# Four moved pieces in a two-block transformer kernel: order of turns in latent attention, low parts of the convolution branch on VectorE, a sum inside a tile, and the first weights between blocks of x

## The reference, cut to what matters

```python
def first_block(x, ...):
    h = rmsnorm(x, norm_in_g)                       # the prologue of the kernel
    proj = h @ w_in                                 # first weight tiles of the ring
    ... stick-breaking attention: y_sb ...
    q = (rmsnorm(c_q) @ w_q_up)                     # 8 heads, 64 + 32 columns each
    kv = (rmsnorm(c_kv) @ w_kv_up)                  # 8 heads, 64 for k and 64 for v
    z = q_full @ k_full.T * scale                   # per head, queries in blocks of 128
    p = softmax(where(allowed, z, -inf))            # key chunk <= query chunk
    o_mla = p @ v_mla
    x = x + (g0 * y_sb + g1 * ((o_mla * silu(gate_mla)) @ w_o_mla)) @ w_out
    return rmsnorm(x, norm_f_g)

def second_block(x, ...):
    ... differential attention a and a causal convolution c of 31 taps ...
    y_a = a @ w_proj_attn
    c = silu(layer_norm(c, conv_ln_w, conv_ln_b))
    y_b = c @ w_proj_conv
    x = x + (sigmoid(g_a) * y_a + sigmoid(g_b) * y_b) @ w_out
    ... feed-forward with silu gate ...
```

## Time and profile before

| | |
|---|---|
| median of three runs | 3171.05 us |
| the profiled execution's own time | 3167.18 us |
| span of its profile | 3165.4 us |
| mean granted TensorE clock | 0.967 of full |
| TensorE busy | 2899.7 us (92%) |
| VectorE busy | 1580.2 us (50%) |
| ScalarE busy | 1228.4 us (39%) |
| GpSimd busy | 750.1 us (24%) |

### The profile page before, as it was taken

The page is one execution under the profiler, slowest core; times in us unless marked ns, Lnnn a source line. Parts: engine busy times, 40 slices in busy tenths (PEclk is TensorE's granted clock), DMA queues, the critical chain, the costliest instruction groups (busy, mean ns, idle before and its releaser), DMA issues. The chain is left out here.

```text
span 3165.4 us, 34002 instructions
## 1 busy us (share of the span) xinstructions
PE 2899.7 (92%) x13392; PEld 2344.9 (74%) x13392; DVE 1580.2 (50%) x1934; ACT 1228.4 (39%) x2019; POOL 750.1 (24%) x330
## 2 busy tenths in 40 slices
PE   6999998977778888999999999978989999999999
PEld 4778887756666766777777777766777888888887
DVE  4566664145675343788888877745332221211121
ACT  4455543224453243565566555535124110111110
POOL 2111121110001231333333333216223222222221
PEclk8999999988999998999999999989999999999999
DMA  4112122113213421211221122244430111111112
GB/s 118 34 54 60 47 67 86 41 28 65 45 37 129 144 80 50 80 46 58 67 62 55 55 67 68 67 179 140 138 115 20 47 47 51 49 47 47 47 47 80
DMA packets 239286, 219.16 MB, mean 69 GB/s; under 512 B 29304, under 2 KB 200856, under 8 KB 239128
## 3 DMA queue, kind: packets, MB, share of 16 engines
q1 hardware_dynamic: 238096, 215.41, 22.1%
q10 hardware_dynamic: 1032, 1.57, 0.3%
HBM read 156.66 MB, written 41.42 MB: 63 GB/s over the span
## 5 line engine op out<-in xcount | busy, mean ns | idle before, releaser
L179 POOL TENSOR_TENSOR w_lo<-w_raw,w_hi 128x1024 fp32r<-128x1024 f32 (+3 forms) x220 | 515.9, 2347 | 1905.6 <-ACT w_hi L171 1905.6
L171 ACT ACTIVATE w_hi<-w_raw 128x1024 fp32r<-128x1024 f32 (+3 forms) x220 | 215.6, 983 | 610.1 <-PE f_banks L239 203.1
L2213 DVE SCALAR_TENSOR_TENSOR d_acc<-d_padded,vectors,d_acc 128x1024 f32<-128x1024 f32 x240 | 389.8, 1624 | 3.0
L209 PE MATMUL d_pp<-h_hi,w_hi 128*128 128x512 f32 x896 | 362.4, 404 | 11.1 <-PEq L67 4.5
L209 PE MATMUL d_pp<-h_hi,w_lo 128*128 128x512 f32 x896 | 362.2, 404 | 0.0
L209 PE MATMUL d_pp<-h_lo,w_hi 128*128 128x512 f32 x896 | 359.9, 402 | 0.0
L239 PE MATMUL f_banks<-h_hi,w_hi 128*128 128x512 f32 x704 | 222.2, 396 | 4.5 <-PEq L67 4.5
L239 PE MATMUL f_banks<-h_lo,w_hi 128*128 128x512 f32 x704 | 221.7, 395 | 0.0
L239 PE MATMUL f_banks<-h_hi,w_lo 128*128 128x512 f32 x704 | 221.6, 395 | 0.0
L209 PE MATMUL s_pp<-h_hi,w_hi 128*128 128x512 f32 x512 | 206.5, 403 | 12.7 <-PEq L67 12.7
L1992 POOL TENSOR_TENSOR d_probs<-d_probs 128x128 f32<-128x128 f32 (+3 forms) x64 | 133.6, 2088 | 338.0 <-ACT d_probs L2108 338.0
(11 more groups left out here) (338 smaller groups left out, 5861.8 us busy)
## 6 DMA issues: line engine op xcount, KB each, us to landing
w_raw<-in_w_in SPq DMA_DIRECT2D x97, 512.0 KB, 3.9
w_raw<-in_w_gate_up SPq DMA_DIRECT2D x44, 512.0 KB, 3.8
w_raw<-in_w_down SPq DMA_DIRECT2D x22, 512.0 KB, 3.6
gates<-s_gate SPq DMA_DIRECT2D x16, 512.0 KB, 5.1
f_gate<-gates SPq DMA_DIRECT2D x16, 512.0 KB, 4.8
w_raw<-in_w_out SPq DMA_DIRECT2D x16, 512.0 KB, 3.7
w_raw<-in_w_proj SPq DMA_DIRECT2D x16, 512.0 KB, 4.9
x_tok_in<-in_x SPq DMA_DIRECT2D x8, 512.0 KB, 7.8
```

The lines of the kernel that those rows point to most:

```text
L171: act.activation(self.hi[:, s, 0:chunks, :], self.raw[:, s, 0:chunks, :], ACT.Copy).then_inc(self.rounded[s], 1)
L179: pool.tensor_tensor(self.lo[:, s, 0:chunks, :], self.raw[:, s, 0:chunks, :], f32(self.hi[:, s, 0:chunks, :]), ALU.subtract).then_inc(self ...
L209: mm = pe.matmul(halves(ps)[h], w[:, k, :], x[:, k, h * HALF:(h + 1) * HALF], start=(k == 0 and r == 0), stop=(k == chunks - 1 and r == 2))
L2213: dve.scalar_tensor_tensor(out=acc[:, :], in0=x, scalar=wt, in1=acc[:, :], op0=ALU.mult, op1=ALU.add).then_inc(c["taps"], 1)
```

## The change

Prologue: SyncE issues the two first weight tiles behind block 3 of x in place of behind block 7, and ScalarE rounds them inside round 7 of its loop, ahead of the last two `h_hi`.

Latent attention: in each step but the second of a head (`at == 1`) the turns of unit s-2 come straight behind the scores, ahead of `fill` and `values`; in the second (`LATE`) they stay behind `values`. The turns of v come at the fifth step (`at == 4`) in place of the seventh, and last in it. ScalarE's roundings and VectorE's subtractions are put in the same order, and so is the numbering `order` of the two banks.

`merge_branches`: the low parts of the convolution's result go from GpSimd (between its tiles 6 and 7 and after 7) to VectorE (all eight in round 6); ScalarE rounds them four at a time one round later than before, apart from the sigmoids; the sum over rows of the squares stands inside tile 4, behind its second chunk, in place of behind tile 3; the reloads of the attention's result are issued one round later.

```diff
-        CONV_V = 6
+        CONV_V, LATE = 4, 1
...
@@ latent attention, ScalarE
+                turned_here = [(s - 2, x) for x in range(CHUNKS[(s - 2) % QB])] if 2 <= s < UNITS + 2 else []
+                if at != LATE:
+                    for u, x in turned_here:
+                        round_t(u, x)
                 if s < UNITS:
                     expose(s)
                 for t, h in halves_at(s):
                     take(t, h)
                 if s >= LAG and (s - LAG) % 2 == 1:
                     copy_low((s - LAG) // 2)
+                if at == LATE:
+                    for u, x in turned_here:
+                        round_t(u, x)
+                if at == CONV_V and head < HEADS_:
+                    for x in range(2):
+                        round_v(head, x)
...
@@ latent attention, TensorE
                 if s < UNITS:
                     score(s)
+                if at != LATE:
+                    for u, x in turned_here:
+                        turn_t(u, x)
                 for t, h in halves_at(s):
                     fill(t, h)
                 if s >= LAG and (s - LAG) % 2 == 1:
                     values(s - LAG)
+                if at == LATE:
+                    for u, x in turned_here:
+                        turn_t(u, x)
                 if at == CONV_V and head < HEADS_:
                     for x in range(2):
                         turn_v(head, x)
-                if 2 <= s < UNITS + 2:
-                    for x in range(CHUNKS[(s - 2) % QB]):
-                        turn_t(s - 2, x)
...
@@ prologue
-            ring.load_ahead(sp)
+                if b == 3:
+                    ring.load_ahead(sp)
...
-            ring.round_ahead(act)
+                if b == TB - 1:
+                    ring.round_ahead(act)
...
@@ merge_branches
-                if u in (5, 7):
+                if u in (6, 8):
...
-                if t in (6, 7):
-                    for k in range(4):
-                        low(k + (4 if t == 7 else 0))
...
+                if t in (5, 6):
+                    for k in range(4):
+                        round_c(k + (4 if t == 6 else 0))
...
+                if t == 6:
+                    for k in range(KC):
+                        low(k)
...
+                    if (t, k) == (4, 1):
+                        pe.wait_ge(c["square_sum"], KC - 1)
+                        add_over_rows(sum2, c["squares_summed"])
```

More of the change, by code:

```diff
@@ L951, in latent_attention @@
             head, at = s // QB + 1, s % QB
+            if 2 <= s < UNITS + 2:
+                order += [("t", s - 2, x) for x in range(CHUNKS[(s - 2) % QB])]
             if at == CONV_V and head < HEADS_:
                 order += [("v", head, 0), ("v", head, 1)]
-            if 2 <= s < UNITS + 2:
-                order += [("t", s - 2, x) for x in range(CHUNKS[(s - 2) % QB])]
         number = {what: i for i, what in enumerate(order)}
@@ L1205, in _ @@
                     norm(s - 1)
[L1206 to L1211, removed]
+                turned_here = [(s - 2, x) for x in range(CHUNKS[(s - 2) % QB])] if 2 <= s < UNITS + 2 else []
+                if at != LATE:
+                    for u, x in turned_here:
+                        low_t(u, x)
                 for t, h in halves_at(s):
@@ L1215, in _ @@
                     add_low((s - LAG) // 2)
+                if at == LATE:
+                    for u, x in turned_here:
+                        low_t(u, x)
+                if at == CONV_V and head < HEADS_:
+                    for x in range(2):
+                        low_v(head, x)
         @block.tensor
@@ L2607, in _ @@
                     invert()
+                if t in (5, 6):
+                    for k in range(4):
+                        round_c(k + (4 if t == 6 else 0))
                 if t in (4, 5):
-                    for k in range(4 * (t - 4), 4 * (t - 4) + 4):
-                        sigmoid_of(k)
-                        if k % 4:
-                            round_c(k - 1)
-                    round_c(4 * (t - 4) + 3)
+                    for k in range(4):
+                        sigmoid_of(k + (4 if t == 5 else 0))
             ring.round_ahead(act)
@@ L2647, in product, with low @@
                                          op0=ALU.add, op1=ALU.mult).then_inc(c["product"], 1)
+            def low(k):
+                dve.wait_ge(c["rounded"], k + 1)
+                dve.tensor_tensor(c_lo[:, k, :], x[:, k, :], f32(c_hi[:, k, :]), ALU.subtract).then_inc(c["low"], 1)
             for k in range(KC):
```

15 lines of the change are left out of this document (1 added, 14 removed).

## The result

The changed kernel takes 3142.18 us (median of four runs, 3140.68 to 3143.81), the kernel before 3169.71 us beside it. The ratio on record is 0.9902, 95% interval [0.9889, 0.9915]: faster by about 1%, where -15 us was forecast. The two medians are 27.5 us apart, which is 0.9913 and inside that interval; 0.9902 itself would be 31 us, and the record does not say where these 3.6 us come from. The profiled execution took 3140.68 us with a span of 3138.9, 26.5 less than before.

What follows compares the result with a forecast made beforehand. TensorE was taken as the bound, busy 2899.7 of 3165.4 us. Prologue +21.5, `merge_branches` -16.5 and latent attention -20 sum to -15.0 us, so 3156 us from a median of 3171.05; range 3132 to 3172.

Steps and rivals of the forecast that it cites:

- Rival (1): Prologue: it doesn't lengthen, since block 4 of x lands early; -38.5 us in all, 3132.5 us; chance 0.12.
- The 1.1 us taken off: `merge_branches`: deducted from its 17.6 us gain because GpSimd's remaining w_lo can stretch VectorE's low parts; left -16.5.
- The "third": `merge_branches`: GpSimd's w_lo can stretch VectorE's low parts by a third, as 2.34 became 3.33 us in the prologue.
- The 5 us taken off: Latent attention: deducted because a waiting turn holds up the half tile, the values and their takers; left -20 us.
- Heads 2 to 5: Latent attention: the longer of two engines' sums per step plus 2.5 us slack per head, a gain of 21 us.
- Heads 1 and 6: Latent attention: a gain of 4 us for both together.
- Heads 7 and 8: Latent attention: nothing changes, as their step is VectorE's.
- The upper end, -34: Latent attention: if heads with half tiles ran like head 7, 28 us less in heads 2 to 5, some 5 elsewhere.
- (2): Latent attention gives only -8 us, as its waits become waits of the turns; total -3, 3168 us; chance 0.17.
- (3): Latent attention: early turns couple the engines, 0.5 us in each of 64 steps; total +12, 3183 us; chance 0.11.
- the likeliest case: Whole kernel: the forecast itself, 3156 us, with its own range of 3143 to 3166; chance 0.60.
- the two signs set for a wrong forecast: Block 4 taken up before 30 us, or the turns' waits in latent attention 20 us more than before.

Runs made afterwards that it cites:

- pro_alone: The kernel before with the prologue's edit alone; 3193.68 us, 1.0071 of the kernel before.
- bias_later: The changed kernel with ScalarE issuing the bias rows in round 4 of the prologue, not before its loop; 3122.73 us, 0.9842 of the kernel before.
- mer_sum3: `no_pro` with the sum over rows of the squares back behind tile 3 in `merge_branches`; 3122.91 us in one run.
- pe_half_last: `no_pro` with TensorE alone turning behind half tile and values in steps with a half tile; 3134.58 us, 0.9875 of the kernel before.
- turns_only: The kernel before with TensorE alone turning right behind the scores in every step, v still at the seventh; 3152.62 us, 0.9931 of the kernel before.
- pe_half_early: `no_pro` with TensorE alone turning behind the values in steps without a half tile; 3124.85 us, 0.9842 of the kernel before.
- no_pro: The changed kernel with the prologue of the kernel before; 3118.45 us, 0.9829 of the kernel before.
- lat_alone: The kernel before with latent attention's edit alone; 3136.69 us, 0.9888 of the kernel before.
- v_fifth_only: The kernel before with the turns of v at the fifth step in place of the seventh; 3170.20 us, 0.9993 of the kernel before.

## Why the prediction was right or wrong

**The prologue: right, in size and in cause.** Block 4 was forecast at 41 us and the next stage near 67.5; it was 41.54 and 68.03. The gain of 2.0 us at the end came as two low parts in 5.62 us without a gap. `pro_alone` gives +22.5 us by itself, and `bias_later` shows the bias rows to be the cause and not the tiles. The Trainium skill ("DMA: Bandwidth & Descriptors", "Queues, rings and completion order") has one row's ring worked off in order, so that x stays behind the tiles; the trace agrees, with block 4 at 41.54 us behind tiles that took up to 35.3 us from issue to landing.

Rival (1) is refuted for this kernel, but is just what happens once no bias rows are in flight.

**`merge_branches`: the mechanism right, the size 2.1 us short.** The 2.8 us of the squares are confirmed by `mer_sum3`. The whole stage as a window, before:

```profile
2109.80:2321.00 211.20, 187.73 (x777) 149.53 (x777) 106.61 (x65) 76.47 (x72) 78.66 (x31) 0.95 0.45 157
```

And after:

```profile
2102.70:2295.30 192.60, 183.03 (x776) 146.95 (x776) 111.33 (x73) 76.45 (x73) 55.53 (x23) 0.97 0.50 172
```

TensorE's busy time fell by 4.7 us, where 4.2 were put down for the clock, and its idle time by 13.9, where 2.8 + 10.6 were. The 1.1 us taken off were not lost: VectorE's low parts did stretch (13.33 us for eight, with 10.2 forecast), but the cover held, with 2.1 us to spare. The "third" that the forecast took from the prologue was the wrong way to size it (see the last section): two of the eight took 3.19 and 3.40 us in place of 1.21, some 4 us and not 1.1.

**Latent attention: the right sign, the size wrong, -30.4 for -20, and the mechanism right in part.** This is the term that failed: 10.4 of the 12.5 us by which the two gains were forecast too small. Split by the forecast's own steps:

- The 5 us taken off because "a turn that waits now holds up the half tile and the values": wrong, and the largest piece. The turns wait as long in all as before (34.2 us, before 33.8), while the half tiles wait 12.4 us less. That a wait in front of the half simply replaces one behind it fits these sums, but no run shows it step by step.
- Heads 2 to 5, laid out at 25.9, 34, 28.4 and 29.3 us: measured 25.1, 33.9, 29.1 and 26.7, a gain of 24.0 and not 21, with nearly all of the difference in head 5.
- Heads 1 and 6, put at 4 us together: 5.3 and 2.5, so 7.8.
- Heads 7 and 8, put at nothing: head 7 lost 1.2 (25.5 for 24.3, at clock 0.93 and not 1.00), head 8 gained 0.2. The way to the first head took 0.4 more.

So 20 + 5 + 3.0 + 3.8 - 1.0 - 0.4 = 30.4. The upper end, -34, was nearer than the middle. It was itself added up wrongly: by the rule that it names (VectorE's busy time plus 3.8, or TensorE's at full clock), heads 3 and 4 come to 30.4 and 26.3 and not 31.5 and 27, which makes it about -35.

The forecast also left out the clock, except that it laid halves out at full speed: 10.8 of the 30.5 us in heads 1 to 7 are busy time at 0.96 for 0.91, 19.7 are idle time.

The reason given, that `m_pp` comes free late in the steps with a half tile, was sound as far as it went: its waits fell by 12.4 us, and putting TensorE's turns back in these steps alone (`pe_half_last`) brings 10.3 us of idle time back. What it missed is that TensorE's order alone does it: the two engines behind took their results in another order than TensorE gave them, and `turns_only` repairs just that and gets two thirds of the gain and 17.4 of the 19.7 us of idle time. That they stood in this way in the steps without a half tile too is not shown; `pe_half_early` has no more idle time than `no_pro`.

**The other rivals.** (2), little gain, is refuted by `lat_alone` (0.9888, upper end 0.9904). (3), slower by coupling, had its price from 0.41 us a step; with the turns' waits at 34.2 us for 33.8, nothing of that price was paid.

**The sum.** +22.0 - 30.4 - 18.6 + 0.5 = -26.5, as the spans have it. The range of 3132 to 3172 held the time, while the likeliest case's own (3143 to 3166) missed it by 0.8 us. The first of the two signs set for a wrong forecast, block 4 before 30 us, did not come, nor the second.

## What to carry to other kernels

When a producer serves two kinds of consumers in a step, compare the order in which it gives with the order in which they take, engine by engine. If ScalarE's first work in a step is TensorE's last, ScalarE stands in between (4.93 us in the step shown), and the stall shows on an engine that looks idle and harmless. Then test which side to move: here moving TensorE's turn forward paid 22 us, while moving the other two back to TensorE's late place gained 12 us in the steps with a half tile and lost 34 in the others. Read a stage's loss as idle time and busy time apart, and beside the ratio of all runs, since one profile's clock can look like a mechanism (`pe_half_early`: 13 us in the profile, 4 in the runs). Lay out each step as the longer of two engines' sums; a deduction on top for "waits that hold up others" needs a row of its own. Before a transfer is moved ahead in a queue, count the packets of everything that shares its engines in that stretch: here 1.5 MB in small packets made an early load of 1 MB cost 22 us, and a later issue of the small packets, with nobody waiting for them, gave 23 back.

## What the runs showed of the hardware

Alone, the bias rows are no faster than beside others. In `bias_later` from 20 to 25 us:

```profile
q10 hardware_dynamic: 168, 0.26, 44.7%
q1 hardware_dynamic: 19, 0.01, 0.8%
```

168 packets in 5 us nearly without company (19 of the other queue), and 164 beside 164 of the weight tiles. So the small packets of the weight tiles went in between nearly free, and what suffered was their own queue alone: on the shared engines its rate was that of the slow one, packet for packet.

TensorE's clock was a third of the latent gain: 10.8 us of 30.5 in heads 1 to 7 are shorter busy time at 0.96 for 0.91 of full, with no work taken away. The sum of the gaps does not set it. `pe_half_early` and `no_pro` are idle 34.0 and 34.4 us and run at 0.90 and 0.97, and `v_fifth_only`, idle some 4 us less than the kernel before, runs at 0.88 where that runs at 0.91. What in these orders lowers the clock stays open.

VectorE and GpSimd waited for each other by whole instructions. Of the eight subtractions of `merge_branches` on VectorE six took 1.21 us each. The two others are those that ran beside one of GpSimd's:

```profile
2190.77 3.19 DVE L2659 TENSOR_TENSOR h_lo<-merged,h_hi 128x1024 fp32r<-128x1024 f32 x1
...
2198.43 3.40 DVE L2659 TENSOR_TENSOR h_lo<-merged,h_hi 128x1024 fp32r<-128x1024 f32 x1
```

```profile
2190.47 2.41 POOL L179 TENSOR_TENSOR w_lo<-w_raw,w_hi 128x1024 fp32r<-128x1024 f32 x1 [10.39 <-ACT w_hi L171]
2197.82 2.93 POOL L179 TENSOR_TENSOR w_lo<-w_raw,w_hi 128x1024 fp32r<-128x1024 f32 x1 [4.95 <-ACT w_hi L171]
```

GpSimd's ended at 2192.88 and 2200.75, VectorE's at 2193.96 and 2201.83, 1.08 us later both times: each looks like a wait for GpSimd's end and then its own work. GpSimd's second took 2.93 for 2.41 us, and it started 0.68 us before a subtraction of VectorE's ended. The prologue of before has the same lengths: 3.33 us for GpSimd's 2.34.
